# Making the next round's key operands earlier and in three places, in a fused two-layer trunk (attention and RWKV-7) on Trainium2

## The chip, the cores and the metric

The kernel is one program on one core of a Trainium2 chip. The metric is the device time of one execution in microseconds, the median of the runs. The core's engines are TensorE (PE, matmuls), VectorE (DVE), ScalarE (ACT), GpSimd (POOL) and SyncE (SP, which only starts DMAs here). Each engine works through a queue of its own in order; they wait for each other on semaphores. The program is written by hand for each engine: nothing reorders it.

## The reference, cut to what matters

Two layers over 256 tokens of width 1024. Each layer projects x into the parts of a sparse multi-query attention, of two gates and of an RWKV-7 time mix, adds the two mixers' outputs through the gates, projects, normalizes, and runs a gated feed-forward. What the change touches is the time mix's key:

```python
w = -jax.nn.softplus(-(w0 + jnp.tanh(p_w) @ w2)) - 0.5
decay = jnp.exp(-jnp.exp(w.astype(jnp.float32)))
a = jax.nn.sigmoid(a0 + p_a @ a2)
kk = hd(k * k_k)                       # 16 heads of 64
kk = kk / jnp.maximum(jnp.linalg.norm(kk, axis=-1, keepdims=True), 1e-12)
k = k * (1 + (a - 1) * k_a)
b_h = kk * a_h
def step(state, inp):
    r_t, w_t, k_t, v_t, kk_t, b_t = inp
    sa = jnp.einsum('bhvk,bhk->bhv', state, -kk_t)
    state = state * w_t[:, :, None, :] + sa[..., None] * b_t[:, :, None, :] + v_t[..., None] * k_t[:, :, None, :]
    return state, jnp.einsum('bhvk,bhk->bhv', state, r_t)
```

In layer 1 v is mixed with layer 0's v by a sigmoid of a small projection.

## The kernel before, in words

The 16 heads are handled in 4 rounds a layer (g = 0 to 3, r = 4 l + g), 4 heads in each: two blocks (GB = 2) of 128 rows that hold two heads each. The 256 steps of the recurrence are cut into 4 chunks of 64, so that a round has 8 units (NU) of two heads by one chunk.

A round on TensorE (`wkv`) is, in order: the grams of the operands `b_of`, `k_of` with `arc` into PSUM banks 2 to 5; V and b turned to token order (`turned_unit`); gaps 0 and 1; k turned (`tokK`, bank 6); gaps 2 and 3; then six levels (1 to 5 in the loop) that invert a triangular matrix by doubling. A level has W for two halves, then XW for two halves, with a copy on ScalarE (`levels`) and a masked update and a transpose on VectorE (`level`) between them. Small products with V run beside them ("side"): `akV` beside W of level 1, `rkV` beside XW of level 1, `ktV` beside W of level 2. Then come four chunk steps c = 0 to 3: Z, Q, S and y, each awaited by a small operation on ScalarE or VectorE. `y_sum` on VectorE ends the round, and the next round's grams wait for it and for the operands.

Other work is put by hand into numbered gaps of a round (`fill(n)`): 14 gaps in the levels, 8 in the chunks. The pieces of the dense projections of x are half a weight block each. A piece needs its weight block split into two rounded parts, `mid_hi` (a cast on ScalarE, line 1143) and `ring_r` (a subtraction on VectorE, line 1462), both called by `mids_up_to`; there are two `mid_hi` buffers. `LEVEL_GAPS` says which gaps of a round hold the 8 pieces of the next round's r and k: 4 to 11 in round 0, and 0 to 7 in rounds 1 and 2. Round 3 has none. The attention's steps have gaps too: logits 4, `y_back` of the round before 7, bonus 8, probabilities 11, values 13. VectorE and ScalarE take in a finished pair in the level that `level_before` gives.

The operands of the next round need these steps: `prep_1` (the decay and a projections, `zw` and `za`) after the levels; `prep_kk` and two tanh (`thw`, `tha`) on ScalarE; `prep_decay` on VectorE (scale, prefix sum, difference); `prep_exp` on ScalarE; `prep_2` on TensorE after y of chunk 0 (in layer 1 the value projection `zv`, then `ss`, the key's sums of squares); `prep_sum` on VectorE, then a power on GpSimd (`head_norm`); `prep_3` after y of chunk 1 (turn of the norm); `prep_rn` on VectorE, in layer 1 with the three v operations; `prep_4` after y of chunk 2 (`rnx`, the norm spread over the rows); and on VectorE in chunk 3 `prep_rest` (kkn, k2, kb, two arc products, b and k operands).

Ahead of a layer's round 0 the same steps stand in another surrounding: TensorE has the attention's index scores, `prep_1`, and 12 dense pieces of the first three gate pairs; VectorE has `prep_decay`, `prep_sum`, and two top-k selections of 8 steps each (`topk`), then `prep_rn`, `prep_rest`.

## Time and profile before

| | us |
|---|---|
| median of 3 runs (1255.3 to 1260.0) | 1255.31 |
| the profiled execution | 1254.65 |
| its span, first to last instruction | 1252.4 |
| TensorE busy in it | 1152.6 |
| VectorE busy | 785.4 |
| ScalarE busy | 539.0 |

The mean granted TensorE clock of the span is 0.977 of full speed. Times in the trace count from the span's start. Layer 0's rounds begin with their grams at 103.75, 168.81, 232.05 and 296.94; layer 1's at 725.92, 790.91, 856.57 and 922.29. A row of the timeline is start, duration, engine, line, operation, output and inputs, count, and, in brackets, how long the engine stood idle before it and whose work ended that. Successive operations overlap a little in their records: the start of the next one tells when the engine was free.

### The profile page before, as it was taken

To read this page: it belongs to the slowest core of one execution; us is meant where nothing else is said; L and a number is where in the kernel's file an instruction comes from. 1 tells how busy PE (TensorE), PEld (TensorE's weight loads), DVE (VectorE), ACT (ScalarE), POOL (GpSimd) and SP (SyncE) were. 2 spreads that over 40 slices of the span, in tenths; PEclk is the share of its full clock that TensorE was granted. 3 is DMA by queue.
4 is the path that set the end of the run, shared out by engine and by line. 5 is a ranking of instruction groups with operands and counts; after the bars stand their busy time and mean duration, and the time that the engine had idled before them with its cause. 6 is when DMAs were issued, how large, how long until landed. Compare 5 with 4: busy or idle time off the path is not lost.

```text
span 1252.4 us, 29267 instructions
## 1 busy us (share of the span) xinstructions
PE 1152.6 (92%) x12328; PEld 1038.1 (83%) x12328; DVE 785.4 (63%) x1436; ACT 539.0 (43%) x938; POOL 54.5 (4%) x56
## 2 busy tenths in 40 slices
PE   7997998997899899999899979989978998999997
PEld 7777887876789799998797768878767897999985
DVE  1267576667476777774512775757584767777745
ACT  2243535353354355553212445353534443555531
POOL 0000000000000100000100000000000001000000
PEclk9999999999999899999999999999999998999998
DMA  7422221211175456556454221212111754555561
GB/s 283 147 90 77 85 91 50 83 52 61 35 260 178 162 178 195 182 195 200 152 179 147 77 73 69 94 53 87 42 53 38 265 170 168 179 192 178 193 200 69
DMA packets 45353, 165.38 MB, mean 132 GB/s; under 512 B 5136, under 2 KB 5392, under 8 KB 44976
## 3 DMA queue, kind: packets, MB, share of 16 engines
q1 hardware_dynamic: 42576, 154.02, 36.6%
q0 software_dynamic: 1504, 7.47, 1.8%
q8 instruction: 98, 1.61, 0.5%
q10 hardware_dynamic: 1152, 2.10, 0.5%
q14 instruction: 23, 0.19, 0.0%
HBM read 160.42 MB, written 3.15 MB: 131 GB/s over the span
## 4 chain that ended last, share of the span: by engine, by line
PE 76%; DVE 16%; issue 3%; ACT 3%; DMA 1%; DVEq 0%; SPq 0%; ACTq 0%
PE ps L700 18%; PE ps L701 16%; PE ps L702 16%; PE ps L836 8%; PE ps L679 5%; PE ps L986 3%; DVE ring_r L1462 2%; PE ps L848 1%; DVE keep L1873 1%; PE ps L1028 1%; DVE small L1871 1%; DMA ring<-stream_dram 1%; DVE X_Y L1577 1%; DVE X_Y L1572 1%; DVE keep L1860 1%
## 5 line engine op out<-in xcount | busy, mean ns | idle before, releaser
L700 PE MATMUL ps<-x_tok_r,mid_hi 128*128 128x256 f32 x448 | 137.7, 307 | 13.7 <-DVE ring_r L1462 12.5
L701 PE MATMUL ps<-xT_r,mid_hi 128*128 128x256 f32 x448 | 127.1, 284 | 0.0
L702 PE MATMUL ps<-x_tok_r,ring_r 128*128 128x256 f32 x448 | 126.9, 283 | 0.0
L700 PEld LDWEIGHTS ps<-x_tok_r,mid_hi 128*128 128x128 f32 x448 | 85.8, 191 | 23.4 <-issue 15.6
L679 PE MATMUL ps<-xT,ring 128*128 128x256 f32 x448 | 99.7, 381 | 0.0
L679 PEld LDWEIGHTS ps<-xT,ring 128*128 128x128 f32 x448 | 84.2, 190 | 13.0 <-issue 1.6
L701 PEld LDWEIGHTS ps<-xT_r,mid_hi 128*128 128x128 f32 x448 | 86.1, 192 | 0.0
L702 PEld LDWEIGHTS ps<-x_tok_r,ring_r 128*128 128x128 f32 x448 | 86.0, 192 | 0.0
L1572 DVE COPY_PREDICATED X_Y<-masks,ps 128x256 f32<-128x256 uint32 x80 | 35.1, 439 | 63.1 <-PE ps L836 55.3
L1462 DVE TENSOR_TENSOR ring_r<-ring,mid_hi 128x1024 fp32r<-128x1024 f32 x56 | 68.0, 1218 | 5.2 <-ACT mid_hi L1143 4.7
L1697 DVE TENSOR_TENSOR w_lo<-ring,w_hi 128x1024 fp32r<-128x1024 f32 x44 | 53.9, 1225 | 26.6 <-ACT w_hi L1178 26.5
L1697 DVE TENSOR_TENSOR rs_ks_r<-ring,tha_kkn_r 128x1024 fp32r<-128x1024 f32 x46 | 56.3, 1225 | 21.4 <-ACT tha_kkn_r L1178 21.4
L1697 DVE TENSOR_TENSOR vs_dC_r<-ring,b_k_r 128x1024 fp32r<-128x1024 f32 x46 | 56.1, 1220 | 17.4 <-ACT b_k_r L1178 17.4
L1697 DVE TENSOR_TENSOR X_Y_r<-ring,arc_r 128x1024 fp32r<-128x1024 f32 x44 | 53.7, 1222 | 21.1 <-ACT arc_r L1178 21.1
L1178 ACT CAST tha_kkn_r<-ring 128x1024 fp32r<-128x1024 f32 x46 | 47.9, 1041 | 33.7 <-PE ps L702 33.7
L1143 ACT CAST mid_hi<-ring 128x1024 fp32r<-128x1024 f32 x56 | 58.7, 1052 | 8.2 <-PE ps L702 8.2
L836 PE MATMUL ps<-X_Y,nT_rb 64*64 64x64 f32 x1280 | 54.2, 225 | 8.2 <-DVE ak_rk L1564 3.1
L1246 ACT COPY W_bt<-ps 128x256 f32<-128x256 f32 x80 | 29.5, 372 | 71.3 <-PE ps L836 51.1
L701 PE MATMUL ps<-oT_r,tha_kkn_r 128*128 128x256 f32 x208 | 59.8, 288 | 0.0
L836 PEld LDWEIGHTS ps<-X_Y,nT_rb 64*64 64x64 f32 x1280 | 44.6, 137 | 17.0 <-DVE X_Y L1572 7.4
L701 PE MATMUL ps<-oT_r,w_hi 128*128 128x256 f32 x208 | 58.4, 281 | 0.0
L701 PE MATMUL ps<-oT_r,arc_r 128*128 128x256 f32 x208 | 58.4, 281 | 0.0
(435 smaller groups left out, 3385.1 us busy)
## 6 DMA issues: line engine op xcount, KB each, us to landing
ring<-stream_dram SPq DMA_DIRECT2D x281, 512.0 KB, 3.5
lora_w<-lora_dram POOLq DMA_DIRECT2D x2, 1536.0 KB, 7.4
W_bt<-rpar_dram POOLq DMA_DIRECT2D x4, 512.0 KB, 5.2
kt_V<-rpar_dram POOLq DMA_DIRECT2D x4, 512.0 KB, 6.0
x_tok<-x_dram SPq DMA_DIRECT2D x2, 512.0 KB, 4.1
v_saved_dram<-vs_dC ACTq DMA_DIRECT2D x4, 256.0 KB, 4.0
x_tok<-x_dram SPq DMA_DIRECT2D x1, 1024.0 KB, 4.8
vf<-v_saved_dram ACTq DMA_DIRECT2D x4, 256.0 KB, 3.9
```

What stands on the lines that cost most here:

```text
L679: mm = pe.matmul(dst[:, b, :], w[:, kb * P:kb * P + P], rhs[:, kb, :], start=(kb == 0), stop=(kb == KB - 1))
L700: pe.matmul(dst, lh, rh, start=start, stop=False)
L701: pe.matmul(dst, lh, rl, start=False, stop=False)
L702: return pe.matmul(dst, ll, rh, start=False, stop=stop)
L836: mm = pe.matmul(dst[q], left[q, u, :], right[q], start=start, stop=stop)
L986: mm = pe.matmul(dst, xT[:, kb, t * P:t * P + P], w[:, kb * P:kb * P + n], start=(kb == 0), stop=(kb == KB - 1))
L1143: act.copy(mid_hi[m % NM][:, :], ring[:, n % RING, :]).then_inc(*act_mid.inc(l, m))
L1178: act.copy(w_hi[m % NS], ring[:, n % RING, :]).then_inc(*act_split.inc(l, m))
L1246: act.copy(W[:, 4 * k:4 * k + 4, :], half64("W", k)).then_inc(*act_wkv.inc(r, f"W{lev}{k}"))
L1462: dve.tensor_tensor(rounded["ring"][:, k, :], ring[:, k, :], f32(mid_hi[m % NM][:, :]), ALU.subtract).then_inc(*dve_mid.inc(l, m))
L1572: dve.copy_predicated(dst[:, 4 * k:4 * k + 4, :], mask_of(which, lev, 4), half64("XW", k)).then_inc(*dve_wkv.inc(r, name))
L1697: dve.tensor_tensor(w_lo[m % NS], ring[:, n % RING, :], f32(w_hi[m % NS]), ALU.subtract).then_inc(*dve_split.inc(l, m))
```

## The change

It does these things:

- `prep_ss` (sums of squares, now PSUM bank 4) moves from chunk 0 to gap 13, ahead of the attention's values; on VectorE it comes ahead of `prep_decay`. ScalarE's `prep_kk` moves to level 4, ahead of `att_pT`.
- The turn of the norm and `zv` move ahead of S of chunk 0; `rnx` moves to chunk 1, between Z and Q.
- VectorE's `prep_rest` is cut into `prep_keys` (chunk 1), `prep_arc` (chunk 2) and `prep_bk` (chunk 3); the v operations go from chunk 2 to chunk 3.
- k is turned beside W of level 1 instead of alone; `akV`, `rkV`, `ktV` each go one half-level later.
- `LEVEL_GAPS` of rounds 1 and 2 become 0, 1 and 4 to 9.
- Ahead of round 0 the order on TensorE becomes `prep_ss`, 2 pieces, `prep_1`, 2 pieces, `prep_v`, 2 pieces, the turn of the norm, 2 pieces, `rnx`, 4 pieces.

```diff
-LEVEL_GAPS = [list(range(4, 12))] + [list(range(8))] * (GROUPS - 2)
+LEVEL_GAPS = [list(range(4, 12))] + [[0, 1] + list(range(4, 10))] * (GROUPS - 2)
+            def prep_ss(r):
+                l, g = divmod(r, GROUPS)
+                if g == 0:
+                    pe.wait_ge(*act_att(l, "qT"))
+                else:
+                    pe.wait_ge(*act_wkv(r - 1, "ktV"))
                 pe.wait_ge(*act_prep(r, "kk2"))
...
-                pe.wait_ge(*act_wkv(r, "Vc"))
-                turned(unit64(6), k_of, OTHER).then_inc(*pe_wkv.inc(r, "tokK"))
                 fill(2)
                 fill(3)
...
-                pe.wait_ge(*dve_wkv(r, "akrk"))
-                pe.wait_ge(*act_wkv(r, "tokK"))
+                pe.wait_ge(*dve_wkv(r, "nTrb"))
...
-                        side = swapped(unit64(5)[:, u, :], ak[:, u, :], Vc[:, u, :])
+                        if u == 0:
+                            pe.wait_ge(*dve_wkv(r, "akrk"))
+                        side = turned_unit(unit64(5), k_of, u, OTHER)
...
                     fill(14 + 2 * c)
+                    if g + 1 < GROUPS and c == 1:
+                        prep_rnx(r + 1)
...
                     fill(15 + 2 * c)
+                    if g + 1 < GROUPS and c == 0:
+                        prep_v(r + 1)
+                        prep_rnT(r + 1)
...
-                    if g + 1 < GROUPS and c < 3:
-                        [prep_2, prep_3, prep_4][c](r + 1)
...
-                for k, p in enumerate((prep_1, prep_2, prep_3, prep_4)):
+                for k, p in enumerate((prep_ss, prep_1, prep_v, prep_rnT)):
                     p(r0)
                     for piece in first[2 * k:2 * k + 2]:
                         piece()
+                prep_rnx(r0)
...
+                    if g + 1 < GROUPS:
+                        gaps[VALUES].append(lambda: prep_ss(r0 + g + 1))
                     gaps[VALUES].append(lambda: att_values(l, g))
...
                         if lev == 4:
+                            if nxt:
+                                prep_kk(r + 1)
                             att_pT(l, g)
                     att_o(l, g)
                     if nxt:
-                        prep_kk(r + 1)
...
+                prep_ss(r0)
                 prep_decay(r0)
-                prep_sum(r0)
+                prep_pend(r0)
                 topk(0)
                 prep_rn(r0)
                 topk(1)
-                prep_rest(r0)
+                prep_keys(r0)
+                prep_arc(r0)
+                prep_v(r0)
+                prep_bk(r0)
...
-                            if nxt:
-                                [prep_sum, prep_rn, prep_rest][c - 1](r + 1)
+                            if nxt and c == 1:
+                                prep_keys(r + 1)
+                            elif nxt and c == 2:
+                                prep_arc(r + 1)
+                            elif nxt:
+                                prep_v(r + 1)
+                                prep_bk(r + 1)
```

## Rows read from the trace of the kernel before

**Rows 1.** The page, part 1.
```profile
PE 1152.6 (92%) x12328; PEld 1038.1 (83%) x12328; DVE 785.4 (63%) x1436; ACT 539.0 (43%) x938; POOL 54.5 (4%) x56
```
**Rows 2.** The waits of TensorE: us in total, times, longest.
```profile
PE ps L836 <- DVE yt L1632: 15.0, 6, 2.5
...
PE ps L818 <- DVE scratch L1686: 6.2, 6, 1.0
PE ps L836 <- DVE b_k L1551: 6.1, 2, 4.1
PE ps L848 <- DVE yt L1649: 3.8, 2, 1.9
...
PE ps L836 <- DVE X_Y L1572: 2.6, 4, 0.7
```
**Rows 3.** Busy time in stretches: length, then by engine; PEclk after POOL.
```profile
168.80:172.80 4.00, 3.98 (x137) 3.93 (x138) 2.61 (x5) 1.03 (x2) 0.00 (x0) 1.00 0.24 91
232.05:236.05 4.00, 4.00 (x104) 4.00 (x107) 1.09 (x3) 0.00 (x0) 0.00 (x0) 0.57 0.22 84
...
922.29:926.29 4.00, 4.00 (x121) 4.00 (x125) 1.25 (x3) 0.00 (x0) 0.00 (x0) 0.64 0.02 4
314.50:317.50 3.00, 3.00 (x25) 1.85 (x22) 2.15 (x4) 2.66 (x11) 0.00 (x0) 0.50 0.00 0
201.10:205.10 4.00, 3.91 (x77) 3.54 (x78) 2.08 (x5) 1.54 (x3) 0.00 (x0) 1.00 0.02 4
```
**Rows 4.** Timeline of ScalarE ahead of layer 0's round 0.
```profile
77.88 0.90 ACT L1190 ACTIVATE tmp<-rs_ks,cpar 128x256 f32<-128x256 f32 x2
78.68 0.82 ACT L1197 ACTIVATE dA<-ps,dpar 128x256 f32<-128x256 f32 x2
```
**Rows 5.** Timeline of TensorE in the same place.
```profile
77.21 0.48 PE L743 MATMUL ps<-lora,lora_w 64*128 64x256 f32 x1
...
78.27 3.72 PE L679 MATMUL ps<-xT,ring 128*128 128x256 f32 x16
...
81.83 0.95 PE L764 MATMUL ps<-const,tmp 128*128 128x2 f32 x8
```
**Rows 6.** Timeline of VectorE in the same place.
```profile
79.54 0.43 DVE L1490 TENSOR_SCALAR dA<-dA 128x512 f32<-128x512 f32 x1
```
**Rows 7.** Timelines of ScalarE and VectorE ahead of layer 1's round 0.
```profile
697.15 0.90 ACT L1190 ACTIVATE tmp<-rs_ks,cpar 128x256 f32<-128x256 f32 x2
...
698.88 0.43 DVE L1490 TENSOR_SCALAR dA<-dA 128x512 f32<-128x512 f32 x1
...
702.94 0.17 DVE L1501 TENSOR_SCALAR ssm<-ps 128x8 f32<-128x8 f32 x1 [0.79 <-PE ps L764]
```
**Rows 8.** Timeline of all engines, round 0, levels 4 and 5.
```profile
138.87 0.80 ACT L1237 COPY scratch<-ps 128x768 f32<-128x768 f32 x1
...
140.26 0.83 DVE L1453 SCALAR_TENSOR_TENSOR rs_ks<-ps,cpar,rs_ks 128x255 f32<-128x255 f32 x2
...
140.43 0.63 PE L836 MATMUL ps<-X_Y,W_bt 64*64 64x64 f32 x16
```
**Rows 9.** The chain in order of time, round 1: start, us, what.
```profile
170.79 0.93 PE ps L848 x64
174.78 1.08 PE ps L848 x32
```
**Rows 10.** Timeline of VectorE, round 1, ahead of level 1.
```profile
174.47 1.21 DVE L1462 TENSOR_TENSOR ring_r<-ring,mid_hi 128x1024 fp32r<-128x1024 f32 x1
```
**Rows 11.** Timeline of ScalarE, round 3, level 2.
```profile
314.14 1.02 ACT L1223 ACTIVATE yt<-ps,cpar 128x256 f32<-128x256 f32 x2 [2.75 <-PE ps L848]
```
**Rows 12.** Timeline of all engines, round 1, chunks 2 and 3.
```profile
223.71 1.15 PE L778 MATMUL ps<-ang,const 8*128 8x128 f32 x8
...
227.52 1.06 ACT L1143 CAST mid_hi<-ring 128x1024 fp32r<-128x1024 f32 x1
...
231.22 0.68 DVE L1632 TENSOR_TENSOR yt<-ps,yt 128x512 f32<-128x512 f32 x1
```

More of the change, by code:

```diff
@@ L494, in trunk @@
                                            + (["thv"] if r >= GROUPS else []) for r in range(R)])
-        dve_prep = Steps(sem("dve_prep"), [["s", "cum", "cp", "pend", "ss", "rnT"]
+        dve_prep = Steps(sem("dve_prep"), [["ss", "s", "cum", "cp", "pend", "rnT", "kkn", "k2", "kb", "arc"]
                                            + (["v1", "v2", "v"] if r >= GROUPS else [])
-                                           + ["kkn", "k2", "kb", "arc", "bneg", "kp", "rkk"] for r in range(R)])
+                                           + ["bneg", "kp", "rkk"] for r in range(R)])
         pool_prep = by_round("pool_prep", ["rn"])
-        pe_wkv = by_round("pe_wkv", ["gramB", "gramK", "V", "tokB", "tokK"]
-                          + sum([[f"W{l}0"] + ["ktV"] * (l == 2) + [f"W{l}1"] + ["akV"] * (l == 1)
-                                 + [f"XW{l}{k}" if l < LEVELS - 1 else f"WtY{l}{k}" for k in range(2)] + ["rkV"] * (l == 1) for l in lv], [])
+        pe_wkv = by_round("pe_wkv", ["gramB", "gramK", "V", "tokB"]
+                          + sum([[f"W{l}0", f"W{l}1"] + {1: ["tokK"], 2: ["rkV"]}.get(l, [])
+                                 + (["XW10", "XW11", "akV"] if l == 1 else ["XW20", "ktV", "XW21"] if l == 2 else
+                                    [f"XW{l}{k}" if l < LEVELS - 1 else f"WtY{l}{k}" for k in range(2)]) for l in lv], [])
                           + sum([[f"Z{c}"] * (c > 0) + [f"Q{c}"] + ([f"S{c}"] if c < NCH - 1 else []) + [f"y{c}"]
@@ L763, in prep_2, with prep_rnT, prep_rnx @@
                         j = 2 * (TT * b + t)
-                        mm = pe.matmul(bank(7)[:, j:j + 2], tmp[:, b, t * P:t * P + P], C["hsel"], start=True, stop=True)
+                        mm = pe.matmul(bank(4)[:, j:j + 2], tmp[:, b, t * P:t * P + P], C["hsel"], start=True, stop=True)
                 mm.then_inc(*pe_prep.inc(r, "ss"))
-            def prep_3(r):
+            def prep_rnT(r):
                 pe.wait_ge(*pool_prep(r, "rn"))
-                pe.transpose(bank(7)[0:8, 128:256], rn[:, :], ident).then_inc(*pe_prep.inc(r, "rnT"))
-            def prep_4(r):
+                pe.transpose(bank(4)[0:8, 128:256], rn[:, :], ident).then_inc(*pe_prep.inc(r, "rnT"))
+            def prep_rnx(r):
                 pe.wait_ge(*dve_prep(r, "rnT"))
-                pe.wait_ge(*act_prep(r, "thv" if r >= GROUPS else "thw"))
                 for b in range(GB):
@@ L924, in wkv @@
                                 w.then_inc(*pe_wkv.inc(r, f"W{lev}{k}"))
-                            if lev == 2 and u < len(step_units):
+                            if lev == 2:
                                 if u == 0:
-                                    pe.wait_ge(*act_wkv(r, "akV"))
-                                v = step_units[u]
-                                side = swapped(unit64(5)[:, u, :], kt[:, v, :], Vc[:, v, :])
-                                if u == len(step_units) - 1:
-                                    side.then_inc(*pe_wkv.inc(r, "ktV"))
+                                    pe.wait_ge(*act_wkv(r, "tokK"))
+                                side = swapped(unit64(5)[:, u, :], rk[:, u, :], Vc[:, u, :])
+                        if lev == 2 and k == 1:
+                            side.then_inc(*pe_wkv.inc(r, "rkV"))
                         if k == 0:
@@ L939, in wkv @@
                             mm = per_head(dst, Y, W[:, u, :], u) if lev < LEVELS - 1 else per_head(dst, W, Y[:, u, :], u)
+                            if lev == 2 and u < len(step_units):
+                                if u == 0:
+                                    pe.wait_ge(*act_wkv(r, "akV"))
+                                v = step_units[u]
+                                side = swapped(unit64(4)[:, u, :], kt[:, v, :], Vc[:, v, :])
+                                if u == len(step_units) - 1:
+                                    side.then_inc(*pe_wkv.inc(r, "ktV"))
                         mm.then_inc(*pe_wkv.inc(r, f"XW{lev}{k}" if lev < LEVELS - 1 else f"WtY{lev}{k}"))
@@ L944, in wkv @@
                     prep_1(r + 1)
-                pe.wait_ge(*act_wkv(r, "ktV"))
+                pe.wait_ge(*act_wkv(r, "rkV"))
                 for c in range(NCH):
@@ L1248, in levels @@
                 if lev == 1:
+                    act.wait_ge(*pe_wkv(r, "tokK"))
+                    act.copy(kt, unit64(5)).then_inc(*act_wkv.inc(r, "tokK"))
                     act.wait_ge(*pe_wkv(r, "akV"))
@@ L1328, in _ @@
                 if l:
-                    prep_tanh(r0, "thv", "hv0", kkn, 6)
+                    prep_tanh(r0, "thv", "hv0", thv, 6)
                 for i in range(1, GATES_FIRST):
@@ L1395, in _ @@
                         if c == 1 and nxt and l:
-                            prep_tanh(r + 1, "thv", "hv0", kkn, 6)
+                            prep_tanh(r + 1, "thv", "hv0", thv, 6)
                         if not nxt and c in (1, 2):
@@ L1914, in _ @@
                     if nxt:
+                        prep_ss(r + 1)
                         prep_decay(r + 1)
@@ L1928, in _ @@
                             chunk_s(r, c)
+                        if nxt and c == 0:
+                            prep_pend(r + 1)
+                            prep_rn(r + 1)
                         mids_up_to(l, mids_by(GAPS * g + 13 + 2 * c))
```

46 lines of the change are left out of this document (25 added, 21 removed).

## The prediction

> **What bounds the kernel now.** I read the page first: TensorE is busy 92% of the span, VectorE 63%, ScalarE 43% [rows 1]. So two things can cost or give time: matmuls that are added to or hidden from TensorE's queue, and the stretches where TensorE stands still. The list of TensorE's waits [rows 2] has the second. The largest is the one this change is about: six times, 15.0 us in all, TensorE waits 2.5 us for `y_sum` (VectorE, line 1632) at the end of a round before it can start the next round's grams. Six more waits of 1.0 us are for the normed attention scores (line 1686), four for the X update of a level (line 1572), two before a layer's first round for `b_k` (line 1551).
>
> That last one is small but tells most: the longer is 4.1 us, so the other is 2.0. Ahead of each layer's round 0 VectorE works from `prep_decay` over the two top-k selections to `b_k`, and TensorE, done with its dense pieces, stands and waits for it. There VectorE sets the end, and each microsecond by which `prep_decay` comes later is one by which the layer ends later.
>
> TensorE's granted clock is the last thing I read [rows 3]. After the 2.5 us wait that ends at 168.81 it stays at 1.00 (2.4 GHz); after the one that ends at 232.05 it is 0.57 in the mean of the next 4 us, so mostly at 1.2 GHz. Four more waits of that kind are followed by such a stretch (the last, at 922.29, by 0.64): five of six. The 1.9 us wait of round 3 (line 1649) is followed by 0.50; a 1.0 us wait that ends at 201.11 is not followed by it, nor are its five fellows. The cost is work at half speed: 4 x (1 - 0.57) = 1.7 us at 232.05, 4 x 0.36 = 1.4 at the mildest. I take 7.7 for the five.
>
> **The change part by part**, against the profiled execution's own 1254.65 us (span 1252.4, 2.25 around it); it lies 0.66 below the median 1255.31, which I neglect.
>
> *1. Start of a layer, both layers: slower.* Before, TensorE issued `prep_1` at once (77.21), then two dense pieces, then `ss`. Now `prep_ss` comes first, then two pieces, then `prep_1`. `prep_ss` waits for `kk2`, which ScalarE makes at 77.88 for 0.90 [rows 4]. TensorE's queue is in order, so everything stands behind it: 78.8, then `ss` 0.95 at most, two pieces 81.83 - 78.27 = 3.56, `prep_1` 78.27 - 77.21 = 1.06 [rows 5], tanh 0.82 on ScalarE (78.68, its row). That is 85.1 for the end of `thw`; VectorE's `prep_decay` waits for it and started at 79.54 [rows 6]. The 16 top-k steps are queued behind it on VectorE and can't pass it. +5.5, less 0.1 for `ssm`, which now goes ahead: +5.4 in layer 0. In layer 1 [rows 7]: 697.15 + 0.90 + 0.95 + 3.56 + 1.06 + 0.82 = 704.4 against 698.88, +5.5, less the 0.8 that VectorE waited for `ss` and its own 0.1: +4.5. Sum +9.9. Nothing hides it.
>
> *2. Round 0 of each layer, levels 4 and 5: slower.* `prep_kk` moves ahead of the copy `pT` on ScalarE. In rounds 1 and 2 the k projection is ready by level 3. In round 0 it isn't: its last pieces are in gaps 10 and 11 still, and VectorE's shift for it starts at 140.26 for 0.83 [rows 8]. Now `kk2` (0.90, from 140.26 + 0.83 = 141.1 to 142.0), `pT` (0.80, to 142.8) and the W copy of level 5 (0.3) come in this order behind it, so level 5's second matmul starts at 143.1, not 140.43: +2.6. `ss` adds 0.3 there. The place it left gives nothing in layer 0 (TensorE waits for S there anyway). Two layers: +5.8.
>
> *3. Levels of rounds 1 and 2: faster.* Turned k, 32 matmuls alone, takes 1.08 on the chain, while V and turned b, 64 matmuls side by side in different quarters of the array, take 0.93 together [rows 9]. Beside W, which leaves the same quarters free, turned k costs between nothing and 1.1; I take 0.1, by the second row. The two pieces between A and level 1 go to gaps 8 and 9, after the rest of level 3's work becomes ready. I followed each engine's queue with its durations from these rows: -1.0 for turned k, -1.5 for the wait for X (2.6 over four, 0.65) and the smaller ones ahead of it at level 3; +0.4 since the piece in level 1 needs `ring_r` (174.47 + 1.21 = 175.7 [rows 10]; wanted at the start of turned k's old place, 174.7, and 0.6 of W behind it), +0.4 because W of level 1 on ScalarE stands behind `y_square`; +1.0 at the normed scores, since `rkv` (0.87) now sits before `att_norm` on VectorE and TensorE arrives earlier; +0.3 for `ss`; -0.6 behind that. I get -1.0 a round, -4.0 for four. Bounds -2.6 (all those waits gone) and +0.5.
>
> *4. Round 3: slightly slower.* `ktV` is done only beside the second XW of level 2, behind `y_back`; ScalarE copies it (0.5) before `y_norm`, which began at 314.14 [rows 11] as soon as `y_back` was done. +0.6, twice: +1.2.
>
> *5. Chunks and the end of a round, six times: faster, but little.* `rnx` (1.15) stood after y of chunk 2, where TensorE would have waited for VectorE's S step and `ring_r` anyway [rows 12]. Before Q of chunk 1, its new place, nothing is awaited: it costs its 1.05 of pitch. Z loses about 0.15 of wait. So y of chunk 3 ends 0.9 later, at 230.4. The VectorE tail is cut by kkn, k2, kb and the two arc products (3.2), but `ring_r` then is late for another reason: its cast on ScalarE (227.52, 1.06) follows Q3 and so comes 0.9 later, to 229.5; `ring_r` (1.2) and `y_sum` (0.7, at 231.22 before) follow: grams at 231.5, not 232.05. -0.55 each, -3.3. In layer 1 the three v operations (2.0) join the tail and still end before that cast. Bounds: 0, and -2.2 if `rnx` is hidden.
>
> *6. Clock.* The wait that is left at the end of a round is 1.1 us. None of the six 1.0 us waits was followed by 1.2 GHz (one of them in [rows 3]). So I count the five slow stretches as gone: -7.7. But there are new waits: some 6 us before the first grams in place of 2.0 and 4.1, as VectorE ends 5 later there and TensorE's pieces 1 to 2 (+1.0 each, bounds 0 and 1.7), 2.9 in round 0 (+1.1 each, its chance times 1.5), 2.0 at the normed scores four times (+0.7 each), 1.5 before the first `ss` (+0.2 each): +7.4 together, bounds 0 and +12. The nearest rows disagree: 2.0 (layer 0's wait for `b_k`) left it up, 1.9 did not, 2.5 did so once in six.
>
> [...]
>
> Sum: 9.9 + 5.8 - 4.0 + 1.2 - 3.3 - 7.7 + 7.4 = +9.3, 1264; I take 1263, as the clock's terms lean high.
>
> **Rivals.**
> *A. The new waits leave the clock up.* Only the two long ones before the grams cost anything: 1254.65 + 1.9 + 2 = 1258.5, no change that can be measured. For it: the 2.0 before layer 0's grams. Against: the 1.9 of round 3. [...]
> *B. Faster: the end of a round closes whole.* If `rnx` in chunk 1 fits into time that TensorE would wait, y of chunk 3 ends no later, the cast isn't late, and the grams start 2.2 earlier, not 0.55: 6 x 1.65 = 9.9 less, and no slow clock after the new waits: 1254.65 + 1.9 - 9.9 = 1247. It decides as soon as `rnx` is followed by its Q with no more delay than before. Against: dense pieces fill chunk 1 on both sides.
> *C. The losses grow.* The preamble's two pieces at 1.2 GHz (3.56 more at most) move `prep_decay` again, and all new waits bring the clock down: +12 to +16, about 1269.
> *D. The change doesn't do what it says in the levels:* gaps 8 and 9 don't cover, -4.0 becomes 0: 1267, within the forecast's own range.
>
> **How the numbers follow.** Forecast with D 0.50, its own range 1260 to 1267; A 0.27 (1255 to 1261); B 0.08; C 0.15. A measurement here can tell 0.5%, 6.3 us, from no change: the line is at 1261.6. Slower: C, and most of the forecast (0.43): 0.58. Same: A and the forecast's lower part: 0.34. Faster: B, 0.08. The range takes in A and most of C: 1254 to 1270.
>
> **What would show it.** Step 1: `prep_decay` of layer 0 near 85, grams near 109; if it stays at 79.5, the largest term is wrong. Step 2: ScalarE's `pT` of round 0 behind two Square instructions, a TensorE wait of 2 to 3 us before W-transposed Y. Step 3: a wait near 2 us before line 818's transposes. Step 5: TensorE's wait for `y_sum` near 1.1, not 2.5. Step 6: slow stretches before the first grams and in round 0, none at the ends of rounds. A time below 1255 would say that steps 1 and 2 are hidden or that step 5 gave far more.

## The result, and the profile after

The changed kernel takes 1281.68 us (median of four runs, 1274.87 to 1290.9) against 1255.83 for the kernel before on the same chip: ratio 1.0203, 95% interval 1.0133 to 1.0273. Run again later (e0) it took 1277.60, ratio 1.0173 (1.0140 to 1.0207). So it is 1.7 to 2.0% slower, 22 to 26 us. Forecast were 1263 us and "slower"; the sign is right, the time lies above the range (1254 to 1270).

The profiled execution took 1283.69 us, span 1281.4, mean granted clock 0.964 (0.977 before). The page, part 1, answers to [rows 1]:

```profile
PE 1159.9 (91%) x12328; PEld 1041.7 (81%) x12328; DVE 786.0 (61%) x1436; ACT 538.7 (42%) x938; POOL 50.6 (4%) x56
```

The same instructions on every engine, 7.3 us more of TensorE's busy time (slower clock) and the rest in waits. TensorE's waits (us in total, times, longest), which answer to [rows 2]:

```profile
PE ps L845 <- DVE b_k L1580: 12.8, 2, 7.3
...
PE ps L845 <- DVE S L1654: 9.9, 24, 0.6
PE ps L827 <- DVE scratch L1715: 9.3, 6, 1.8
...
PE ps L845 <- ACT W_bt L1267: 7.0, 6, 2.5
PE ps L845 <- DVE nT_rb L1593: 6.4, 4, 1.7
PE ps L845 <- DVE yt L1661: 6.2, 6, 1.0
```

The wait for `y_sum` (yt) fell from 15.0 to 6.2 us: the change does what it says there. In its place `b_k`, ahead of the two first grams, rose from 6.1 to 12.8, the normed scores (scratch) from 6.2 to 9.3, and two waits are new: 2.5 for W of level 5 on ScalarE in round 0, and the one for `nT_rb` ahead of level 1 in the rounds that have no dense piece there. The chunk steps pay as well. In the kernel before, the products of `prep_2` to `prep_4` stood where TensorE would have waited for VectorE's S; now they stand earlier, and TensorE waits for S in every round:

```profile
PE ps L836 <- DVE S L1625: 2.4, 6, 0.6
```

That is the kernel before; 9.9 now. Of the 8.8 us that the `y_sum` waits lost, 7.5 came back here.

The start of layer 0, TensorE, then ScalarE and VectorE (answers to [rows 4 to 6]):

```profile
78.28 1.13 PE L1067 MATMUL ps<-kiT,arc 128*128 128x256 f32 x4 [0.49 <-ACT scratch L1345]
81.06 1.02 PE L774 MATMUL ps<-const,tmp 128*128 128x2 f32 x8 [1.65 <-ACT tmp L1211]
81.94 5.39 PE L682 MATMUL ps<-xT,ring 128*128 128x256 f32 x16
87.26 0.48 PE L746 MATMUL ps<-lora,lora_w 64*128 64x256 f32 x1
```
```profile
80.02 0.90 ACT L1211 ACTIVATE tmp<-rs_ks,cpar 128x256 f32<-128x256 f32 x2
88.42 0.84 ACT L1218 ACTIVATE dA<-ps,dpar 128x256 f32<-128x256 f32 x2 [7.51 <-PE ps L749]
```
```profile
89.29 0.43 DVE L1512 TENSOR_SCALAR dA<-dA 128x512 f32<-128x512 f32 x1 [7.01 <-ACT dA L1218]
```

What to look for is the order of step 1 of the prediction (`kk2`, `ss`, two pieces, `prep_1`, tanh, decay) and one number that it didn't have: the two pieces take 5.39, not 3.72 [rows 5]. They run at half clock.

Windows at the places that [rows 3] show for before (length, busy by engine, PEclk after POOL): first grams of layer 0; after the new wait at level 5 of round 0; grams of rounds 1 and 2; behind the normed scores of round 2:

```profile
113.33:117.33 4.00, 4.00 (x124) 4.00 (x128) 1.43 (x3) 0.00 (x0) 0.00 (x0) 0.65 0.01 4
155.20:159.20 4.00, 4.00 (x36) 3.76 (x36) 1.58 (x2) 1.17 (x2) 0.00 (x0) 0.74 0.00 0
185.33:189.33 4.00, 4.00 (x137) 3.93 (x138) 2.60 (x5) 1.74 (x3) 0.00 (x0) 1.00 0.50 175
247.75:251.75 4.00, 4.00 (x137) 3.93 (x138) 2.61 (x5) 1.74 (x3) 0.00 (x0) 1.00 0.49 175
279.80:283.80 4.00, 4.00 (x68) 3.76 (x63) 1.97 (x5) 1.33 (x3) 0.00 (x0) 0.57 0.01 4
```

Slow clock left the ends of rounds and came to the start of the layer, to round 0 and behind the normed scores.

Where the 29.0 us between the two spans lie, from the start times of the grams, of `prep_1` and of the last index scores in the two timelines (before, after):

| stretch | layer 0 | layer 1 |
|---|---|---|
| last index scores to first grams | 27.6, 35.1: +7.4 | 30.5, 37.2: +6.7 |
| round 0, grams to `prep_1` | 39.5, 47.0: +7.5 | 38.6, 47.4: +8.8 |
| round 0, `prep_1` to next grams | 25.5, 25.0: -0.5 | 26.4, 26.7: +0.3 |
| round 1 | 63.2, 62.4: -0.8 | 65.7, 65.4: -0.2 |
| round 2 | 64.9, 63.5: -1.4 | 65.7, 67.5: +1.8 |
| round 3 to the next index scores, or the end | -0.8 | -1.9 |

That makes 26.9; the other 2.1 are ahead of layer 0's index scores, where nothing is changed (x arrives 1.0 later, and slow first matmuls). The two starts and the two rounds 0 hold 30.2; all the rest together is 3.3 shorter.

The profile of e0, the same kernel once more, is 21.7 longer than that of before. Counted in the same way, its two starts cost 12.4, its rounds 0 15.7, and 2.4 lie ahead; the other rounds gain 8.8. So the losses repeat, and the size of the gain does not: in the first profile round 2 of layer 1 took 67.5, in e0 64.3, as the clock was down behind the normed scores for 10 us (granted clock 0.50 from 918.3 to 928.5).

### The profile page after: what moved, and what is told of

It is laid out like the page before. It is cut to its first block, busy times and chain, and to the rows that moved or that the text cites. A ratio compares the mean times of both kernels' runs of the same rounds, so it can differ in the third digit from the quotient of the medians.

```text
span 1281.4 us, 29259 instructions
## 1 busy us (share of the span) xinstructions
PE 1159.9 (91%) x12328; PEld 1041.7 (81%) x12328; DVE 786.0 (61%) x1436; ACT 538.7 (42%) x938; POOL 50.6 (4%) x56
## 4 chain that ended last, share of the span: by engine, by line
PE 75%; DVE 17%; issue 3%; ACT 3%; DMA 1%; DVEq 0%; SPq 0%; ACTq 0%
PE ps L703 17%; PE ps L704 16%; PE ps L705 16%; PE ps L845 8%; PE ps L682 5%; PE ps L1004 3%; DVE ring_r L1484 2%; DVE keep L1902 1%; PE ps L1046 1%; DVE small L1900 1%; PE ps L857 1%; DMA ring<-stream_dram 1%; PE ps L746 1%; PE ps L774 1%; DVE X_Y L1606 1%
## 5 line engine op out<-in xcount | busy, mean ns | idle before, releaser
L703 PEld LDWEIGHTS ps<-x_tok_r,mid_hi 128*128 128x128 f32 x448 | 86.1, 192 | 30.1 <-issue 16.8
L682 PE MATMUL ps<-xT,ring 128*128 128x256 f32 x448 | 103.3, 390 | 0.0
L1726 DVE TENSOR_TENSOR w_lo<-ring,w_hi 128x1024 fp32r<-128x1024 f32 x44 | 53.9, 1225 | 26.7 <-ACT w_hi L1199 26.6
L845 PE MATMUL ps<-X_Y,nT_rb 64*64 64x64 f32 x1280 | 56.9, 232 | 7.6 <-DVE nT_rb L1593 6.4
L704 PE MATMUL ps<-oT_r,b_k_r 128*128 128x256 f32 x208 | 58.2, 280 | 0.0
```

The costliest lines, as they stand in the source:

```text
L682: mm = pe.matmul(dst[:, b, :], w[:, kb * P:kb * P + P], rhs[:, kb, :], start=(kb == 0), stop=(kb == KB - 1))
L703: pe.matmul(dst, lh, rh, start=start, stop=False)
L704: pe.matmul(dst, lh, rl, start=False, stop=False)
L845: mm = pe.matmul(dst[q], left[q, u, :], right[q], start=start, stop=stop)
L1726: dve.tensor_tensor(w_lo[m % NS], ring[:, n % RING, :], f32(w_hi[m % NS]), ALU.subtract).then_inc(*dve_split.inc(l, m))
```

## The experiments

All ratios are to the kernel before on the same chip, with 95% intervals. 0.1% is 1.26 us. "From" names the kernel that was edited; kernels in different groups ran on different chips, so they are compared by their ratios. A median of few executions and the ratio can differ by some us: e5's median is 19 above its kernel before, its ratio says 17.

| run | from | median us | ratio (interval) |
|---|---|---|---|
| e0 | after | 1277.6 | 1.0173 (1.0140-1.0207) |
| e1 start of layer undone | after | 1261.9 | 1.0044 (1.0023-1.0066) |
| e2 kk2 of round 0 undone | after | 1268.2 | 1.0097 (1.0066-1.0129) |
| e3 both undone | after | 1251.4 | 0.9981 (0.9960-1.0002) |
| e4 kk2 of round 0 alone | before | 1262.7 | 1.0059 (1.0040-1.0078) |
| e5 start of layer alone | before | 1275.2 | 1.0134 (1.0099-1.0169) |
| e6 long wait filled | after | 1283.5 | 1.0222 (1.0190-1.0254) |
| e12 wait before sums filled | after | 1275.3 | 1.0163 (1.0137-1.0189) |
| e13 both waits filled | after | 1274.4 | 1.0156 (1.0120-1.0192) |
| e8 round 0's parts undone | e3 | 1251.4 | 0.9957 (0.9934-0.9979) |
| e15 turned k alone | e8 | 1255.1 | 0.9989 (0.9965-1.0014) |
| e16 old gaps | e8 | 1254.3 | 0.9994 (0.9977-1.0011) |
| e11 scores normed first | e8 | 1249.6 | 0.9949 (0.9930-0.9968) |
| e10 V, b before the grams | e8 | 1248.9 | 0.9942 (0.9920-0.9964) |
| e17 e10 and e11 | | 1246.7 | 0.9920 (0.9891-0.9949) |
| e18 e17, wait filled | e17 | 1245.7 | 0.9916 (0.9884-0.9948) |

**Undoing the two suspects (e1, e2, e3).** e1 gives the start of the layer its old order:

```
-for k, p in enumerate((prep_ss, prep_1, prep_v, prep_rnT)):
+for k, ps in enumerate(((prep_1,), (prep_v, prep_ss), (prep_rnT,), (prep_rnx,))):
...
-prep_ss(r0); prep_decay(r0); prep_pend(r0)     # VectorE
+prep_decay(r0); prep_pend(r0); prep_ss(r0)
```

> The changed kernel with the start of both layers put back in its old order (prep_1, two dense pieces, then the norm's sums; on VectorE the decay steps first). Theory (half of the loss is the start of the layer: the norm's sums ahead of prep_1 and of two pieces hold up VectorE's chain to the first grams): TensorE's wait before the first grams falls from 5.5 and 7.4 us to under 3.5 and 4.5, the stretch from last index scores to first grams from 35.1 and 37.2 us to 28 and 31, and the time by 12 to 17 us, to 1265 to 1270. Rival 1 (the three-step split of the key operands holds the first grams, in whatever order they start): the stretches stay above 33 us and the time above 1277. Rival 2 (the clock's slow stretches only move): the waits go back but the time falls by less than 6 us.

The stretches to the first grams fell to 27.6 and 30.5, exactly those of before, `b_k` waited 6.1 us in all, and the time fell by 1.3 to 1.6% (against e0 and against the first measurement), 16 to 20 us, where 12 to 17 were expected. Round 0 stayed as long as in the changed kernel (72.4, 73.1). Rivals 1 and 2 fall.

e2 puts round 1's `kk2` behind the levels of round 0, and its sums behind `prep_1`:

```
 if lev == 4:
-    if nxt: prep_kk(r + 1)
+    if nxt and g != 0: prep_kk(r + 1)
     att_pT(l, g)
 att_o(l, g)
+if nxt and g == 0: prep_kk(r + 1)
```

> The changed kernel with the square of round 1's keys (kk2) back behind the levels of round 0, and its sums (prep_ss) behind prep_1 there; rounds 1 and 2 and the start of the layer stay as changed. Theory (ScalarE's kk2 at level 4 of round 0 holds the copy of W of level 5, TensorE waits 2.45 us and comes back at half clock): that wait falls under 1.0 us, the time from round 0's grams to those of round 1 falls from 72.0 and 74.1 us to 65 to 67, and the time by 8 to 16 us, to 1266 to 1274. Rival 1 (round 0 is long because its grams follow the long wait at the start of the layer and run at half clock): round 0 gains 2 to 3 us in each layer, the time falls by 4 to 6 us. Rival 2 (kk2 is late for the chunks and waits there instead): no change over 2 us.

The wait of 2.5 for W of level 5 is gone, round 0 fell to 68.8 and 68.5 (from 72.0 and 74.1), the time by 0.8 to 1.1%, 9 to 14 us. The theory's mechanism holds, but its 65 to 67 for round 0 was missed: round 0 is still 3.5 to 3.7 longer than before. Something else is in it.

> Both edits of the two runs above together: old order at the start of the layers, kk2 and its sums behind the levels in round 0, changed order in rounds 1 to 3. Theory: what is left of the change is the part that gains (levels of rounds 1 and 2, chunks, round 3), 1248 to 1254, level with the kernel before (1255.8) or 0.5% faster. Rival 1 (the gains do not add up, the clock takes them): 1256 to 1264. Rival 2 (something not undone here, such as turned k beside level 1, costs time): above 1264.

What is left of the change is level with the kernel before: 0.2% less, with an interval that just touches none. The two suspects together explain the loss. Round 0 was 67.6 and 68.9 against 65.1 and 65.0; all other rounds were shorter than before.

**The same two from the other side (e4, e5).** From the kernel before, each suspect alone.

```
 if lev == 4:
+    if g == 0: prep_kk(r + 1)      # e4; taken out behind the levels there
     att_pT(l, g)
```

> The kernel before with one edit: in round 0 the square of round 1's keys (prep_kk) goes ahead of the copy pT on ScalarE, as the change has it; nothing else is changed. Theory (ScalarE's kk2 holds the copy of W of level 5): a TensorE wait of about 2.5 us before W-transposed Y in both layers, round 0 longer by 3 to 5 us each, part of it at half clock; the time 6 to 10 us above the kernel before, 1261 to 1265. Rival (by the prediction's own figure, 2.6 us each and no clock cost): 1259 to 1260.5. Rival 2 (the waits that follow in the chunks take it in): under 3 us, 1255 to 1258.

+0.6% (7.4 us), and TensorE waits 2.45 in both layers. Round 0 is 69.0 and 69.5, +4.0 and +4.5, but the clock stayed at 1.00 behind the wait, in layer 0 (145.20) and in layer 1 (770.02), and not "part of it at half clock" as the theory had it:

```profile
145.20:149.20 4.00, 3.93 (x53) 3.23 (x53) 2.02 (x3) 1.75 (x3) 0.00 (x0) 1.00 0.00 0
770.00:774.00 4.00, 3.91 (x53) 3.21 (x53) 2.02 (x3) 1.77 (x3) 0.00 (x0) 1.00 0.00 0
```

Measured from the grams to the matmul behind the wait and compared with before, the wait itself costs 2.6 in each layer (40.6 against 36.7, less 1.3 that TensorE was late already; in layer 1 40.2 against 35.7, less 1.8). The 1.3 and 1.8 lie ahead of the edit's place: near the start of round 0 the clock was down for longer in this execution (0.50 from 113.0 to 119.8; before, only to 116.2). No wait of the edit stands there, so they are the execution's, and the edit's own cost is 5.2, at the lower end of the interval (5.0 to 9.8).

After the full change the clock was 0.74 at the same place. Seven profiles have this wait, twice each (the changed kernel's, e0, e1, e6, e12, e13 and e4). In the first six the sums `ss` come soon behind it, and the clock went down within 2.0 us after its end in all twelve places. In e4 no sums follow, and it went down in neither. That the sums, narrow matmuls, make the difference is not shown: the six kernels differ from e4 in more than this.

e5 is the kernel before with the changed order at the start of the layer (sums, two pieces, `prep_1`; sums, rn and its broadcast in bank 4 there).

> The kernel before with only the start of the layers in the changed order (the norm's sums, two dense pieces, then prep_1; VectorE takes the sums' maximum ahead of the decay steps). Theory (undoing it took 20 us off the changed kernel, 14 of them between the last index scores and the first grams): waits of 5.5 and 7.4 us before the first grams, and 14 to 20 us more than the kernel before: 1268 to 1275. Rival (only the prediction's 9.9 us; the rest came from an interplay with the other parts): 1263 to 1267.

+1.3% (16.8 us). The stretches were 36.7 and 37.2; round 0 grew by 1.6 and 2.7 as well, with nothing changed in it: the grams behind the long wait run at half clock, 3.7 in both layers against 2.0 and 2.5 before. 0.59 + 1.34 is 1.93%, about the whole loss.

**Is it the wait or the clock? (e6, e12, e13)** Matmuls of 256 columns into a free bank, result unused, in TensorE's waits at the start of the layer.

```
+for _ in range((16, 24)[l]):        # e6: ahead of the first grams; e13: (10, 14)
+    pe.matmul(bank(2)[:, 0:T], ident, xT[:, 0, :], start=True, stop=True)
...
+for _ in range((7, 3)[l]):          # e12 and e13: ahead of prep_ss, bank 5
```

> The changed kernel with 16 (layer 0) and 24 (layer 1) matmuls of 256 columns into a free bank while TensorE waits for the first grams; by the dense pieces' rows they take 3.7 and 5.6 us at full clock, and the waits are 5.5 and 7.4 us. Their result is not used. Theory (the clock comes back low after these waits and makes grams and what follows slow): granted clock near 1.0 at the first grams, grams under 2.0 us of each group instead of 3.3 and 3.7, round 0 shorter by 2.5 to 5 us in each layer, time 1272 to 1277. Rival 1 (the low clock in round 0 has another cause, the short waits in the levels): no change of over 2 us. Rival 2 (they run at half clock and end behind the wait): 1282 to 1288.

The run missed its theory, as the filling was sized wrongly. TensorE's timeline, layer 0:

```profile
108.66 7.07 PE L1081 MATMUL ps<-xT,const 128*128 128x256 f32 x32
115.66 0.33 PE L845 MATMUL ps<-arc,b_k 64*64 64x128 f32 x2
```

The 16 matmuls stand in the trace as 32, since each is done in two passes; 16 of a trace's matmuls, two dense pieces, take 3.7 us, so these take 7.07 at full clock, twice what was expected, and overran the wait of 5.5. The sizes in the expectation of e13 are to be doubled too. The grams behind them ran at full clock and round 0 was 0.9 and 2.6 shorter. The overrun is seen from `prep_1` to the grams: +1.4 and +2.9. The whole stretches grew by 3.0 and 1.3, since the clock ahead of `prep_1` differed as well. In layer 0 the sums and the two pieces were both slow and took 1.7 more than in the changed kernel's profile, in layer 1 the pieces were fast (3.70) and took 1.7 less:

```profile
80.36 1.72 PE L774 MATMUL ps<-const,tmp 128*128 128x2 f32 x8 [1.65 <-ACT tmp L1214]
81.94 6.35 PE L682 MATMUL ps<-xT,ring 128*128 128x256 f32 x16
```

The time is rival 2's without its cause.

> The changed kernel (1281.7) with 7 (layer 0) and 3 (layer 1) matmuls of 256 columns into a free bank between the last index scores and the first sums (prep_ss), where TensorE waits 1.65 us for kk2; their result is not used. Theory (this wait brings the clock down, and the two dense pieces behind it take 5.25 us instead of 3.56, so that prep_1 and VectorE's chain to the first grams are 1.7 us later): the pieces at 3.6 to 4.2 us, first grams 1 to 1.7 us earlier in layer 0, time 1278 to 1280.5. Rival 1 (the clock falls there for the thin work before it, index scores and waits, not for this wait): no change, 1281 to 1283. Rival 2 (the matmuls themselves run at half clock and delay the sums): 1283 to 1285.

```profile
78.50 3.19 PE L1074 MATMUL ps<-xT,const 128*128 128x256 f32 x14
81.52 0.95 PE L774 MATMUL ps<-const,tmp 128*128 128x2 f32 x8
82.33 3.70 PE L682 MATMUL ps<-xT,ring 128*128 128x256 f32 x16
85.96 0.48 PE L746 MATMUL ps<-lora,lora_w 64*128 64x256 f32 x1
```

With the wait for `kk2` filled the two pieces take 3.70, not 5.39 as in the timeline of the changed kernel above. The 3.19 of matmuls are longer than the wait of 1.65, so the sums start 1.2 later behind the last scores (81.52 - 77.53 against 81.06 - 78.28), and layer 0's stretch is 0.55 shorter in the end, not 1 to 1.7. The time is 0.1 to 0.4% below the changed kernel's, within their intervals; that it lies below the expected 1278 says little, since e0 does too.

One pair of places would not settle rival 1, as the clock is not the same in every execution. All profiles together do. Five have the wait of 1.65 unfilled (the changed kernel's, e0, e2, e5, e6), ten places: the pieces behind it were slow in eight (5.30 to 6.37) and fast in two (3.70, layer 1 of e0 and of e6). With it filled (e12, e13) they were fast in four of four. The thin work before it is the same in all. Rival 1 falls. Whether it is the idle time alone, or the idle time with the narrow sums behind it, was not tried.

> The changed kernel with matmuls of 256 columns into a free bank in both waits at the start of a layer: 7 and 3 before prep_ss, as in the run that took 1275.3 us, and 10 and 14 in the wait before the first grams (2.2 and 3.1 us at full clock, 4.4 and 6.2 at half, in waits of 5.5 and 7.4). Their result is not used. Theory (half clock at the first grams and what follows is a cost of its own): the grams of layer 0 and 1 take 2.0 us instead of 3.5 and 3.7, first grams start no later, round 0 is 2 to 3 us shorter in each layer, time 1269 to 1272. Rival (the waits of 1.8, 0.8 and 2.3 us behind the grams bring the clock down again whatever it was before): the grams alone gain, 1.5 us each, time 1272 to 1275. Rival 2 (no gain, slow clock only moves): 1275 to 1278.

First grams at full clock in both layers:

```profile
111.65:115.65 4.00, 2.91 (x128) 2.77 (x128) 2.73 (x5) 1.04 (x2) 0.00 (x0) 1.00 0.01 4
742.49:746.49 4.00, 2.91 (x128) 2.77 (x128) 2.73 (x5) 2.29 (x4) 0.00 (x0) 1.00 0.17 57
```

Round 0 is 1.2 and 1.4 shorter than in e12 (71.1, 72.3 against 72.3, 73.7), as the rival had it: the gain is that of the grams and the turned operands right behind them. The median is the rival's too, 1 us below e12's, and the ratios (0.07% apart) do not tell the two from each other. So of the 17 us that the start of the layers costs the clock's part is the smaller: 1.7 for each pair of pieces that runs slow (5.39 to 3.70), 2.6 at the two first grams; the rest is the longer chain.

**What is left in round 0, and what the rest is worth (e8, e15, e16).** e8 is e3 with round 0's parts in their old places, in code `if g in OLD:` around the two orders, OLD = (0,).

> The kernel with both edits undone (1251.4) and in addition round 0's parts beside the levels as before: turned k by itself ahead of level 1, ak V beside W and rk V beside XW of level 1, kt V beside W of level 2. Rounds 1 to 3 stay as changed. Theory (round 0 has no dense piece ahead of level 1; without turned k TensorE stands 1.75 and 0.95 us there and comes back at half clock, and level 1 gets longer): round 0 from 67.6 and 68.9 us to 66.2 and 65.8, time 1246 to 1249. Rival (the first dense piece of round 0 starts 9.21 us after the grams in both kernels, so turned k is hidden in either place, and only the clock's luck differs): 1250 to 1252.

The ratio is 0.24% under e3's (3 us), the theory's size, but the intervals overlap and the median, 1251.4, is the rival's. Round 0 is 66.2, as the theory had it, and 67.7 where 65.8 was expected. The profiles tell more. In layer 0 the grams run at full clock in both kernels, and from them to `prep_1` e8 takes 39.4 (39.5 in the kernel before) and e3 40.9. The windows show why. e3, behind the grams and at level 1 of round 0, then e8 at the same places:

```profile
109.00:113.00 4.00, 1.50 (x30) 1.35 (x31) 4.00 (x4) 0.37 (x1) 0.00 (x0) 0.50 0.00 0
116.00:120.00 4.00, 4.00 (x75) 3.44 (x75) 0.44 (x1) 0.86 (x2) 0.00 (x0) 0.65 0.01 4
```
```profile
110.00:114.00 4.00, 0.71 (x33) 0.60 (x33) 4.00 (x4) 0.52 (x2) 0.00 (x0) 0.96 0.00 0
117.00:121.00 4.00, 4.00 (x86) 3.53 (x85) 0.90 (x2) 0.86 (x2) 0.00 (x0) 0.99 0.00 0
```

Round 0 has its first dense piece inside level 1, and it starts 9.2 us after the grams in both (VectorE's `ring_r` is late). Turned k by itself stood in that hole for nothing and kept TensorE at work; beside level 1 it stands partly behind it. Layer 1: 41.0 in e8, 42.2 in e3. Each is one execution, and the clock is part of the difference, so 1.2 to 1.5 is the size and not a bound.

> The same kernel of 1251.4 us with rounds 1 and 2 as well given the old parts: turned k by itself ahead of level 1 instead of beside it (key norm, gaps of the dense pieces and chunk steps stay as changed). Theory (turned k beside level 1 is nearly free, alone it takes 1.08 us): 1.0 us more in each of four rounds, 1254 to 1257. Rival (the order beside the levels is the same work for TensorE, and a wait behind it takes the difference): 1250 to 1253.

+0.32% over e8 (4.0 us), the theory's size, though the intervals overlap. The rounds in which the clock stays up show it without them: 63.3 against 62.4 in layer 0 (e15's round 1, e8's round 2) and 64.2 against 63.3 in layer 1 (e15's round 2, e12's round 1), 0.9 a round. In rounds 1 and 2, where dense pieces cover the hole, turned k beside W is worth what the prediction gave it.

> The same kernel of 1251.4 us with the dense pieces of rounds 1 and 2 back in gaps 0 to 7 (four ahead of level 1), all else the same. Theory (moving two pieces behind level 3 hides waits of 0.65 and some at level 3, but puts the shift rkv ahead of att_norm and gives 0.8 of it back at the normed scores): within 3 us either way, 1250 to 1254. Rival (the moved pieces are worth the 1.5 us a round that the prediction gave them): 1256 to 1259.

+0.37% (4.6 us) over e8. The median, 1254.3, is just above the theory's range and under the rival's, though the wait at the normed scores is back at 1.0 in it. But it isn't quite the old order: with turned k gone from its place, `bonus` comes early for `y_norm`, a wait that neither kernel has at this size:

```profile
PE ps L815 <- ACT yt L1289: 5.6, 6, 0.9
```

Where the clock stays up, a round takes 64.1 against 62.4 in layer 0 and 65.0 against 63.3 in layer 1, 1.7 more. That holds `bonus`'s wait of 0.9 too, so it bounds the moved pieces from above: at most 1.7 us a round. In the time it is 1.2 a round, as the waits of 1.8 and the slow clock behind them are gone in e16.

**Versions that beat both (e11, e10, e17, e18).**

```
 if lev == 3:
     bonus(r)
+    att_norm(l, g)                  # e11, VectorE
 for t in range(2): ... rkv(l, g + 1, t)
-if lev == 3: att_norm(l, g)
```

> The kernel with both edits undone and round 0's parts as before (1251.4), with one more edit: on VectorE the attention scores are normed (att_norm) ahead of the k projection's shift (rkv) at level 3 of rounds 1 and 2; the change had put rkv there. Theory (the wait before the normed scores' transposes is 1.8 us four times because of it, and half a microsecond of slow clock follows): the wait returns to 1.0 us, the time falls 3 to 5 us, to 1246.5 to 1248.5. Rival (kk2 on ScalarE, queued ahead of the last W, is what then ends last: it needs the projection that VectorE now shifts 0.9 us later): no change, 1250 to 1252.

The wait fell to 1.0 as expected (6.2 over six), the time by 0.1% against e8, not told apart from none. A wait for X of a level (3.1 over four) took part of its place.

```
+if g in (1, 2, 3): turn_vb()        # V and turned b, e10
 pe.wait_ge(*dve_y(r - 1, "y"))
 for u in range(NU): ... gram_b, gram_k
-turn_vb()
```

A second edit is in e10: in round 0 the turn of the norm goes behind y of chunk 0.

> The kernel of the third of these runs with two more edits: in rounds 1 to 3 the turning of V and b goes ahead of the grams, into the wait of 1.0 us for y_sum; in round 0 the transpose of rn goes behind y of chunk 0 (it waited 0.7 us for GpSimd). Theory: the 1.0 us waits at six ends of rounds and 0.7 us at two go, 6 to 7 us less than the run before it: 1240 to 1243. Rival (what then comes late is VectorE's gram masks and X, for which the 1.15 us of turning was cover): within 2 us of it, 1246 to 1250. Slower if the grams' end is late for VectorE's queue.

0.15% under e8, the rival's result, and not told apart from none. The rounds with the clock up are 0.4 shorter (62.07 against 62.44), and round 0 of layer 0 is 1.0 shorter behind `prep_1` by the second edit (25.75 against 26.74). The `y_sum` wait is gone from the list, but 1.9 of it came back at `ak_rk` (3.5 for 1.6), and in round 3, which has no dense piece ahead of level 1, the cover of 1.1 us for `nT_rb` is missing:

```profile
PE ps L855 <- DVE nT_rb L1654: 5.3, 2, 2.7
```

> The kernel with V and b turned ahead of the grams (1248.9) with the scores normed ahead of rkv as well (which was worth 1.7 us with a wide interval by itself): theory 1245.5 to 1248, under both kernels; rival (the two share one slack, kk2 and the last W on ScalarE end last at level 5): 1248 to 1250.

0.8% faster than the kernel before (10 us), and 2.5 to 2.8% faster than the changed one. Its rounds 1 and 2 take 62.0, 62.0, 62.9, 62.9 us, with the clock up in all four.

> The same with 4 (layer 0) and 9 (layer 1) matmuls of 256 columns into a free bank in the waits of 2.0 and 4.1 us before the first grams; their result is not used. Theory (in layer 1 the grams come at half clock, 3.7 against 2.0 us, and turned V and b 2.0 against 1.1): 2 to 3 us less, 1243 to 1246. Rival (the waits before round 0's first dense piece bring the clock down anyway): within 1 us. Rival 2 (they run at half clock and delay the grams): 1 to 2 us more.

In layer 1 the grams' window reads 1.00 where e17's reads 0.64, and they take 2.0, not 2.7; round 0 is 1.2 and 0.9 shorter; the median only 1.0 less, 0.04% in the ratio, which is the rival's result. The clock's share is seen in the profiles and is too small for the times to tell it from none.

```profile
720.81:724.81 4.00, 3.31 (x141) 3.18 (x143) 2.73 (x5) 2.30 (x4) 0.00 (x0) 1.00 0.19 60
```

> The changed kernel as it is, for its own median beside the other runs. Expected 1279 to 1284 with a spread of over 8 us from lowest to highest, against one of 8 for the kernel before; a median under 1277 would mean that the first measurement was high by luck, and that the edits' gains are to be read lower.

The second measurement is 4 us below the first and just under what was expected, with a spread of 4.3, not over 8. The effects of the edits are therefore given against both. The two profiles show one source of such differences: in layer 1, same code, same wait of 1.65, the two pieces took 3.70, not 5.39, and the stretch 35.5, not 37.2. The larger one is round 2 of layer 1, 64.3 and 67.5.

```profile
710.82 1.02 PE L774 MATMUL ps<-const,tmp 128*128 128x2 f32 x8 [1.65 <-ACT tmp L1211]
711.71 3.70 PE L682 MATMUL ps<-xT,ring 128*128 128x256 f32 x16
```

## Why the forecast was too low by 15 to 19 us

The prediction's terms by place, beside what the two profiles of the changed kernel show:

| place | forecast | first profile | e0 |
|---|---|---|---|
| ahead of the first index scores' end | 0 | +2.1 | +2.4 |
| two starts (step 1, clock 0.4) | +10.3 | +14.1 | +12.4 |
| rounds 0, grams to `prep_1` (step 2, clock 4.2) | +10.0 | +16.3 | +16.2 |
| rounds 0, the rest (step 5) | -1.1 | -0.2 | -0.5 |
| rounds 1 to 3 (steps 3 to 6) | -9.9 | -3.3 | -8.8 |
| sum | +9.3 | +29.0 | +21.7 |

The step that failed is the one for round 0, +10.0 forecast and +16.2 to 16.3 measured: it is the largest miss in e0, it repeats, and e2, e4 and e8 take it apart. The start of the layer is next. The gain of the later rounds came nearly as forecast in e0, and a third of it in the first profile.

*The term that was missing: turned k in round 0.* The prediction walked the queues of rounds 1 and 2 and of round 3, and carried over only `kk2` and `ss` to round 0; what the new place of turned k costs there was put at nothing without a reason. In round 0 the piece gaps start in level 1, so nothing stands between the turned operands and level 1. In layer 0 TensorE waits 1.75 and 0.80 there, where before it waited 0.69 and 1.05 and had turned k between; it comes back at 1.2 GHz, and level 1 holds the turning besides. Of the +7.5 and +8.8, e2 gives 3.9 and 4.6 to `kk2` with the clock behind it (its 4.9 and 5.6 less the sums' 1.0, which it moves too), 2.6 of them the wait itself (e4). 1.2 and 1.4 are the grams' clock (e13), 1.5 and 1.2 turned k (e8), and 1.0 each is `ss`. Forecast were 2.6 for the wait, 1.1 for the clock behind it, 1.0 for the grams' clock, 0.3 for `ss` and 0 for turned k.

*Step 2 (round 0, +5.8): the wait right, `ss` too small.* The wait of 2.45 and its cost of 2.6 are what was forecast. That e4's time came out at 7.4, the 5.2 of the two waits and the 2.2 of clock, is luck: behind these waits the clock stayed up in e4, and what it lost by the clock lies elsewhere.

*Step 1 (start of a layer, +9.9, and +2.0 of clock): the mechanism right, the size too small.* From last scores to the end of `thw` it forecast 9.0 us; it took 11.0 in layer 0. 1.8 of the 2.0 is one term: the two pieces were taken at 3.56, from [rows 5], where TensorE came to them at full clock; now they stand behind a wait of 1.65 and run at half clock, 5.39. That possibility stood in the prediction as rival C and as a bound, and was not in the sum. From decay to grams is 24.2 before and 24.0 after: the rest of the chain was read rightly. The stretches cost +7.4 and +6.7 (+7.5 and +5.0 in e0) for +5.4 and +4.5. With the grams' clock the whole step costs 17 us by e5 (12 to 21 by its interval), 12 were forecast.

*Step 3 (rounds 1 and 2, -4.0): turned k right, `ss` and a gain behind it wrong.* From grams to `prep_1` round 1 of layer 0 went from 37.7 to 37.5, -0.2 for -1.0. Turned k is worth 0.9 (e15). The waits came much as forecast: 1.5 us of them are gone, 0.3 for `ring_r`, 0.4 for W and 0.8 at the normed scores are new, for the 0.4, 0.4 and 1.0 of the prediction. But `ss` was costed at 0.3: its own row showed 0.95 [rows 5], TensorE has no gap there, and it takes 1.05 in the new place (at 219.62). The prediction's last term, -0.6 "behind that", has no row, and nothing in the profile answers to it.

*Step 4 (+1.2)* was not tried by itself. Round 3 in the whole was 0.8 and 1.9 shorter than before, but before it had slow grams, which cost 1.6 each: the step is neither confirmed nor refuted.

*Step 5 (-3.3): right where the clock is up.* Wait 1.0 for 1.1; `prep_1` to grams 25.55 to 24.95 in round 1 of layer 0, -0.60 for -0.55. Over the six it is -1.6 in the first profile, where the clock is down at `prep_1` in two rounds of layer 1, and -2.9 in e0. The wait for `y_sum` lost 1.5 a round and the round's end only 0.6, as TensorE waits for S instead. Rival B is out.

*Step 6 (clock, -7.7 and +7.4): the first half right, the second too low.* The slow stretches at round ends went; each had cost 1.6 (round 2 of layer 0 64.9 with one, round 1 63.2 without). Behind the 1.8 us waits at the normed scores new ones came in three of four, in both profiles of the changed kernel. They cost 1.1 where the clock soon came back (63.5 against 62.4) and 3.3 once (67.5 against 64.3 in e0), forecast 0.7. The other slow stretches came to the start of the layer and to round 0, where the time at half clock makes the chain later. Time at 1.2 GHz in the span, by the mean granted clock (twice its distance from 1, times the span): 58 us before, 92 after, 79 in e0, 65 in e3, 35 in e18.

Rival A (the clock stays up after waits of 1.5 to 2.9 us) is refuted by the eight slow places of ten behind the wait of 1.65, and by e12. The Trainium skill, "TensorE: Matmul & The Clock Gate", section "HAM oscillation — how this bites in real kernels", has a rule against idle gaps, all longer than this one, and beside it a kernel in which micro-idles between groups of matmuls make the clock go up and down. By the rule alone the clock would stay up behind 1.65 us; this trace disagrees with that, and is nearer to the second. The wait is not the whole cause either: the same wait in e0's layer 1 left the clock up.

Still open: why the same wait takes the clock down in one execution and not in the next. The 1.1 and 2.7 us by which round 0 of e8 is longer than before are placed, if not all explained. In layer 0 they lie behind `prep_1` (26.7 against 25.5), where the turn of the norm waits 0.7 for GpSimd; with the turn moved (e10) it is 25.8. In layer 1 2.4 lie ahead of `prep_1` (41.0 against 38.6), with slow grams (3.6 against 2.5); e18, whose grams run at full clock, has 39.5.

## What to carry to other kernels

A reordering that gains in the steady rounds must be walked through the first round and the start of the phase with their own queues: here the later rounds gained 3 to 9 us together, and the first ones and what leads up to them lost 28 to 30. An operation that stands in a hole costs nothing where it is; ask what fills the hole before it is moved. And a duration taken from a row holds for the clock that the row had: if the change puts a wait ahead of it, cost it at both levels. When a wait is cut, ask which wait the work that stood in its shadow now uncovers: 15.0 us of waits for `y_sum` became 6.2, and those for S went from 2.4 to 9.9.

## What the runs showed of the hardware

The key's sums, four f32 matmuls of two columns that stand as eight in the trace, each with its weight load, take 0.95 to 1.05 us at full clock, as long as turning an operand with 32 matmuls of the trace (1.08 [rows 9]). An f32 matmul stands in the trace as two: 16 of 256 columns are 32 there and take 7.07 us at full clock.

What followed TensorE's waits, by the granted clock of all eighteen profiles: after 1.0 us (at the normed scores and for `y_sum`) it never went down, in over a hundred places. After 1.8 us at the normed scores it went down in 24 of 44. After 1.65 us ahead of the sums and dense pieces, in eight of ten; with the wait filled by unused matmuls, in none of four (5.39 to 3.70). After 2.45 us with the sums soon behind it, in twelve of twelve; after 2.45 us without them, in neither of two. So the length of the wait alone does not tell it here.
